# Three orders in a two-block transformer kernel: convolution taps in other loops around the gates, a merge tile's high and low parts at the head of the next step, key reciprocals spread by transpositions

## The chip, the cores and the metric

The kernel runs on one core of one Trainium2 chip. The metric is the device time of one execution in microseconds (us); smaller is better. The engines are TensorE (PE; its weight loads are listed apart, as PEld), VectorE (DVE), ScalarE (ACT), GpSimd (POOL) and the queue of SyncE (SP), which issues most of the transfers.

## What is computed

Two transformer blocks on 512 positions of width 1024. Cut to the parts that the change touches:

```python
# first block, token mixer
z = h @ w_in + b_in
q, k, v, glu_a, glu_b, gate_a, gate_b = jnp.split(z, splits, axis=-1)
a = chunked_rel_attention(q, k, v, rel_bias) @ w_attn_o
u = glu_a * jax.nn.sigmoid(glu_b)                    # 512 channels
u = causal_dwconv(u, w_dw, b_dw)                     # 31 taps in each channel
u = jax.nn.silu(layer_norm(u, g_ln, b_ln))
cb = u @ w_conv_o + b_conv_o
y = jax.nn.sigmoid(gate_a) * a + jax.nn.sigmoid(gate_b) * cb
return y @ w_mix_o
# second block, recurrence: keys divided by their norm in each head
kk = hd(k * k_k)
kk = kk / jnp.maximum(jnp.sqrt(jnp.sum(kk * kk, axis=-1, keepdims=True)), 1e-12)
# second block, merge of its two branches: again sigmoid(gate) * branch, summed, then a 1024x1024 product
```

Everything is float32. A large product is made of three passes of a faster format: both operands are cut into a high part and a low rest, and the matmuls high x high, high x low and low x high are added.

## The kernel before

All activations are kept with channels on the 128 partitions and the 512 positions along the row, so a width of 1024 is 8 tiles (DT = 8). Weights come in units of 128x1024 (one output tile of a product) through a ring of four slots; a slot's next load is issued when PE has used the unit in it. ACT or POOL makes a unit's high part and POOL its low part. The instruction stream of each engine is written out by hand, and the engines meet only through semaphores; what stands in a row on one engine runs in that order, and a wait holds back all that is behind it.

**Front and convolution (40 to 150 us).** PE makes the 8 tiles of the gated linear unit, then 12 units of queries, keys and values. `gate(g)` exists on ACT (the sigmoid) and on DVE (the product and the first tap with the bias). It is there for four tiles of channels, 0 to 3. Channels 1, 2 and 3 take their 30 further taps on DVE: `tap` is one `scalar_tensor_tensor` on a PSUM bank that must wait for the tap before it in the same channel; `taps_on(n, *channels)` is a loop of n rounds with one tap for each channel named, as (channel, first tap). Channel 0 takes 26 taps in pairs whose products ACT makes (`act_tap_pair`) and POOL adds (`pool_tap_pair`), and its last four on DVE (L1188). Then DVE sums the channels (L1197 to L1203), PE adds over partitions with a matrix of ones (L977), DVE centres (L1208), ACT squares, DVE sums again (L1213), PE's second L977 follows, then root and reciprocal (L1216). PE stands behind both L977: the first is behind unit 9 of the 12, the second behind unit 10. DVE also has four modulation products (L1444) between L1213 and L1216. Attention begins on PE at L689, behind unit 11.

**Merges (`act_mix`, `dve_mix`, `pe_mix`).** For each of 8 tiles n PE makes four half or whole products in PSUM, ACT two sigmoids (L1495), DVE two products and their sum y[n] (L1526, L1528, L1531). `first_part(n)` on ACT makes the high part Y_HI (L1488), `second_part(n)` on DVE the low part Y_LO (L1519). In the first block's merge ACT also makes high parts of weights (L866) and DVE four modulation products a step. The product that follows (mixo1, mixo2) reads y tile by tile: `pe_first_units_split` does tiles 0 to 6 of unit 0, then two tiles of unit 1, then tile 7 of unit 0, and `y_ready(k)` is its wait ahead of tile k of unit 0.

**Recurrence, preparation (`pe_rprep`, 826 to 982 us).** For each of 8 tiles PE makes three units (L2349 to L2351) and between them small products: `key_spread(j)` turns DVE's reciprocals, laid out by position, back to channels with four 128x128 matmuls against the identity (L2326). DVE's L2477 waits for them.

Of the kernel before, what the change touches and what calls it, by code (L numbers as in the profile page):

```python
# [181 lines left out]
def build_program(nc, stream, cols, const, onehot, c_rows, x_t, mem_t, line1, table2, w2a2, g2, cmp_w2, out, scratch, rows):  # L182

    with ExitStack() as ctx:
# [677 lines left out]
        def act_front_high(act, u):  # L862

            slot = u % W_SLOTS
            act.wait_ge(w_full[slot], 16 * (u // W_SLOTS + 1))
            nc.scalar.activation(FHI[:, slot, :], W[:, slot, :], ACT.Copy).then_inc(f_whi, 1)  # L866
# [115 lines left out]
        def act_front(act):  # L982
# [46 lines left out]
            act.dma_start(scratch[1, 0:H2, :], line2[:, 0:LINE]).then_inc(s_line2, 16)  # L1029
            for n in range(4):  # L1030
                act_tap_pair(act, n)
            gate(2)
            act_front_high(act, 4)
            act_tap_pair(act, 4)
# [62 lines left out]
        def dve_front(dve):  # L1097
# [80 lines left out]
            gate(1)  # L1178
            taps_on(10, (1, 1))
            gate(2)  # L1180
            taps_on(10, (1, 11))
            gate(3)
            taps_on(10, (1, 21), (2, 1), (3, 1))
            taps_on(20, (2, 11), (3, 11))
            for t in range(TAIL_TAPS):
                at = CONV_K - TAIL_TAPS + t
                dve.wait_ge(l_vec, t) if t else dve.wait_ge(s_cv[0], 1)
                V.scalar_tensor_tensor(psum[0][:, :], GLU[:, 0, LEAD - CONV_K + 1 + at:LEAD - CONV_K + 1 + at + S],  # L1188
                                       prm("w_dw_conv", at), psum[0][:, :], ALU.mult, ALU.add).then_inc(l_vec, 1)
# [286 lines left out]
        def act_mix(act, stage, per, bias_a, bias_b, y, hi):  # L1476
# [12 lines left out]

            for n in range(DT):  # L1490
                act.wait_ge(s_ev, e0 + n - 1)
                for h, bias in enumerate((bias_a, bias_b)):
# [4 lines left out]
                    if per == 3 and n < DT - 1:  # L1497
                        for m in ((4,), (5, 6))[h]:
                            if 3 * n + m < 3 * DT:
                                act_front_high(act, u0 + 3 * n + m)  # L1500
                if n:
                    first_part(n - 1)
                if per == 3 and n + EARLY < ADA_LATE // 4:
# [6 lines left out]
        def dve_mix(dve, stage, per, y, bias, hi, lo):  # L1510
# [9 lines left out]

            for n in range(DT):
                dve.wait_ge(s_glu, g0 + 2 * n + 2)
                dve.wait_ge(unit_done, u0 + per * (n + 1))
                t = SQ[:, 2 * (n % 2), :]
                v = SQ[:, 2 * (n % 2) + 1, :]
                nc.vector.tensor_tensor(t, psum[4 * (n % 2) + 1][:, :], t, ALU.mult).then_inc(s_dve, 1)  # L1526
                b = 0.0 if bias is None else prm(bias, n)
                nc.vector.scalar_tensor_tensor(v, psum[4 * (n % 2) + 3][:, :], b, v, ALU.add, ALU.mult)\  # L1528
                    .then_inc(s_dve, 1)
                dve.wait_ge(s_dve, d0 + 2 * (n + 1) + max(0, n - 1))  # L1530
                nc.vector.tensor_tensor(y[n], t, v, ALU.add).then_inc(s_ev, 1)  # L1531
                if n:
                    second_part(n - 1)
                if per == 3 and n + EARLY < ADA_LATE // 4:
                    late_modulation(dve, n + EARLY)
# [171 lines left out]
        def pe_ffn1(pe):  # L1707
            mixed = BASE["mix1"]

            def y_ready(k):  # L1710
                pe.wait_ge(s_dve, mixed.dve + min(3 * k + 5, 3 * DT))

# [599 lines left out]
        def pe_rprep(pe):  # L2312
# [10 lines left out]
            def key_spread(j):  # L2323
                pe.wait_ge(m_rec, j + 1)
                for b in range(S // P):
                    last = nc.tensor.matmul(psum[5][:, b * P:(b + 1) * P], TMP[7][:, b * P:(b + 1) * P], con("ident"),  # L2326
                                            start=True, stop=True)
                last.then_inc(m_wide, 1)
# [459 lines left out]
        def pe_cross(pe):  # L2788
            base, mixed = BASE["cross"], BASE["mix2"]

            def y_ready(k):
                pe.wait_ge(s_dve, mixed.dve + 2 * DT + min(3 * k + 5, 3 * DT))

# [708 lines left out]
```

## Time and profile before

| | |
|---|---|
| time, median of 3 runs | 2260.36 us (2259.55 to 2262.89) |
| profiled execution, its own time | 2267.29 us |
| its span | 2265.5 us |
| PE busy | 2201.3 us, 97% of the span |
| DVE, ACT, POOL busy | 1162.1, 775.2, 1211.4 us |
| mean granted clock of TensorE | 0.992 of full speed |

An engine is busy while an instruction of it runs; matmuls are pipelined, so their listed length (0.39 us) is more than the distance between the starts of two of them (0.23 us for 512 columns). A row of a timeline gives start, length, engine, line and instruction, and in brackets the idle time ahead of it with what ended that time.

### The profile page before, as it was taken

The page shows a single profiled execution, that of the slowest core. Times are in us where ns is not written, and L with a number is a line of the kernel's source. Part 1 is how long each engine was busy: PE and PEld are TensorE (multiplying, and loading weights), DVE is VectorE, ACT ScalarE, POOL GpSimd, SP SyncE. Part 2 cuts the span into 40 slices and gives each one's busy share as a digit, 9 for nine tenths or more (in the row PEclk, how much of TensorE's full clock was granted, in tenths as well). Part 3 has the DMA queues.
Part 4 walks back from the last instruction along what each step waited for, and adds up shares of the span by engine and source line. Part 5 has one row for each costly group of instructions (what it writes and reads, how often), then busy time and mean ns, then how long its engine had stood idle before and what let it go on. Part 6 is the DMA issues. An engine that isn't in the chain of part 4 may idle for free.

```text
span 2265.5 us, 40352 instructions
## 1 busy us (share of the span) xinstructions
PE 2201.3 (97%) x16228; PEld 1730.8 (76%) x16228; DVE 1162.1 (51%) x1719; ACT 775.2 (34%) x1355; POOL 1211.4 (53%) x681
## 2 busy tenths in 40 slices
PE   9989999999999999998879998999999999999999
PEld 4857877888888767788876575668887788888887
DVE  7885656555520467753335526673217637555500
ACT  5455322433310266533324225771002242323200
POOL 1955454688877300000006454568877458777776
PEclk9989999999999999999999998999999999999999
DMA  8533652333323332220002240002334212323322
GB/s 330 165 133 112 234 194 84 116 102 93 97 97 93 98 125 75 84 79 4 4 4 75 75 168 19 2 1 93 101 95 137 84 48 93 101 93 100 95 93 102
DMA packets 65425, 220.77 MB, mean 97 GB/s; under 512 B 6913, under 2 KB 9226, under 8 KB 65282
## 3 DMA queue, kind: packets, MB, share of 16 engines
q1 hardware_dynamic: 51072, 179.81, 24.6%
q10 hardware_dynamic: 9986, 24.82, 3.0%
q0 software_dynamic: 4224, 14.06, 1.8%
q8 instruction: 111, 1.82, 0.3%
q14 instruction: 32, 0.26, 0.0%
HBM read 213.09 MB, written 11.86 MB: 99 GB/s over the span
## 4 chain that ended last, share of the span: by engine, by line
PE 73%; POOL 11%; issue 9%; DVE 5%; ACT 1%; DMA 1%; DVEq 0%; POOLq 0%; SPq 0%; ACTq 0%
PE banks L498 12%; PE banks L499 12%; PE banks L500 12%; POOL WH L451 5%; POOL WL_A L454 3%; PE banks L2113 3%; PE banks L2068 3%; PE banks L746 2%; PE banks L689 2%; PE banks L707 2%; PE banks L2349 2%; PE banks L2350 2%; PE banks L2351 2%; PE banks L905 2%; PE banks L906 2%
## 5 line engine op out<-in xcount | busy, mean ns | idle before, releaser
L451 POOL TENSOR_TENSOR WH<-W,ZERO 128x1024 fp32r<-128x1024 f32 x194 | 368.6, 1900 | 280.2 <-PE banks L500 247.3
L454 POOL TENSOR_TENSOR WL_A<-W,WH 128x1024 fp32r<-128x1024 f32 x138 | 339.4, 2460 | 10.9
L498 PE MATMUL banks<-HF,WH 128*128 128x512 f32 x704 | 275.9, 392 | 0.1
L499 PE MATMUL banks<-HF,WH 128*128 128x512 f32 x704 | 273.9, 389 | 0.0
L500 PE MATMUL banks<-HF,WL_A 128*128 128x512 f32 x704 | 273.9, 389 | 0.0
L488 POOL TENSOR_TENSOR WH<-W,ZERO 128x1024 fp32r<-128x1024 f32 x20 | 41.2, 2058 | 277.8 <-DVEq L399 204.6
L872 POOL TENSOR_TENSOR WR_LO<-W,FRONT_HI 128x1024 fp32r<-128x1024 f32 x40 | 96.0, 2406 | 128.8 <-ACT FRONT_HI L866 87.2
L498 PEld LDWEIGHTS banks<-HF,WH 128*128 128x128 f32 x704 | 132.2, 188 | 28.2 <-POOL WL_A L454 0.5
L500 PEld LDWEIGHTS banks<-HF,WL_A 128*128 128x128 f32 x704 | 132.2, 188 | 27.6
L499 PEld LDWEIGHTS banks<-HF,WH 128*128 128x128 f32 x704 | 132.2, 188 | 27.3 <-issue 0.2
L454 POOL TENSOR_TENSOR WL_C<-W,WH 128x1024 fp32r<-128x1024 f32 x56 | 141.7, 2530 | 4.4
L498 PE MATMUL banks<-HID,WH 128*128 (+1 forms) x352 | 137.4, 390 | 0.9 <-POOL WL_A L454 0.9
L499 PE MATMUL banks<-HID,WH 128*128 (+1 forms) x352 | 137.0, 389 | 0.0
L500 PE MATMUL banks<-HID,WL_A 128*128 (+1 forms) x352 | 136.9, 389 | 0.0
L1639 DVE TENSOR_TENSOR HID<-SQ,HID 128x512 f32 x44 | 98.0, 2227 | 41.0 <-ACT HID L1596 41.0
L498 PE MATMUL banks<-HN_HI,WH 128*128 128x512 f32 x288 | 115.6, 402 | 0.8 <-issue 0.4
L499 PE MATMUL banks<-HR,WH 128*128 128x512 f32 x288 | 112.3, 390 | 0.0
L1617 DVE SCALAR_TENSOR_TENSOR SQ<-banks,PRM,SQ 128x511 f32<-128x511 f32 x66 | 49.4, 748 | 115.2 <-ACT SQ L1589 114.6
L3234 POOL DMA_DIRECT2D BIG<-g x1 | 0.5, 532 | 198.0 <-DVEq L399 198.0
L1589 ACT ACTIVATE SQ<-banks,PRM 128x512 f32<-128x512 f32 x66 | 51.2, 776 | 127.5 <-PE banks L500 84.3
L844 POOL TENSOR_SCALAR BIG<-BIG,SM,GT 128x128 f32<-128x128 f32 (+3 forms) x96 | 60.7, 644 | 57.6 <-DVE SM L806 57.6
L1526 DVE TENSOR_TENSOR SQ<-banks,SQ 128x512 f32<-128x512 f32 x16 | 11.1, 691 | 154.7 <-PE banks L500 123.8
(499 smaller groups left out, 5333.0 us busy)
## 6 DMA issues: line engine op xcount, KB each, us to landing
W<-stream SPq DMA_DIRECT2D x308, 512.0 KB, 3.5
BIG<-stream ACTq DMA_DIRECT2D x30, 512.0 KB, 5.3
BIG<-stream SPq DMA_DIRECT2D x20, 512.0 KB, 11.4
bias_rows<-bias_lines POOLq DMA_DIRECT2D x1, 4096.0 KB, 18.9
X<-x_t SPq DMA_DIRECT2D x2, 1024.0 KB, 7.6
BIG<-stream SPq DMA_DIRECT2D x2, 1024.0 KB, 11.8
bias_rows<-bias_lines POOLq DMA_DIRECT2D x1, 2048.0 KB, 16.1
BIG<-bias_rows POOLq DMA_DIRECT2D x1, 2048.0 KB, 11.2
```

Source lines behind the costliest of these rows:

```text
L451: nc.gpsimd.tensor_tensor(WH[:, half, :], W[:, slot, :], ZERO[:, 0:1].to_broadcast([P, D]), ALU.add)\
L454: nc.gpsimd.tensor_tensor(WL[stage][half], W[:, slot, :], WH[:, half, :], ALU.subtract)\
L498: nc.tensor.matmul(out_ap, w_hi, hi, start=start, stop=False)
L499: nc.tensor.matmul(out_ap, w_hi, lo, start=False, stop=False)
L500: return nc.tensor.matmul(out_ap, w_lo, hi, start=False, stop=stop)
L844: ins = nc.gpsimd.tensor_scalar(p, p, SM[:, 32 + m:33 + m], part["gate"][c], ALU.mult, ALU.mult)
L872: nc.gpsimd.tensor_tensor(WR_LO[:, slot, :], W[:, slot, :], FHI[:, slot, :], ALU.subtract).then_inc(f_wlo, 1)
L1589: nc.scalar.activation(SQ[:, 2 * j + h, :], psum[2 * j + h][:, :], ACT.Identity, scale=taps(w, off + j, i, 2), bias=PRM[:, bass.ds(C0[b] + ...
L1617: nc.vector.scalar_tensor_tensor(t[:, 1:S], bank[:, 0:S - 1], taps(w, off + j, i, 1), t[:, 1:S], ALU.mult, ALU.add).then_inc(s_dve, 1)
L1639: nc.vector.tensor_tensor(HIDS[1][:, 2 * i + j, :], SQ[:, 2 * j, :], HIDS[0][:, 2 * i + j, :], ALU.subtract).then_inc(s_ev, 2)
L2068: return nc.tensor.matmul(out_ap[to:to + CHUNK, :], lhs(at, j), rhs(at, j), start=start, stop=stop)
L2113: last = nc.tensor.matmul(one_bank(b)(j)[lo:lo + CHUNK, :], lhs[1](lo, j), rhs[1](lo, j), start=True, stop=True)
```

## The change

On DVE the rounds of the tap loops are distributed otherwise, and five taps of channel 3 stand singly between the last four of channel 0. On ACT two tap pairs go behind the sigmoid of gate 2. In the merges the high and low parts of tile n-1 stand at the head of step n, and PE's wait for tile k asks for the parts up to k. The four matmuls of the key spread become four transpositions.

```diff
@@ act_front
-            for n in range(4):
+            for n in range(2):
                 act_tap_pair(act, n)
             gate(2)
+            for n in range(2, 4):
+                act_tap_pair(act, n)
             act_front_high(act, 4)
@@ dve_front
             gate(1)
-            taps_on(10, (1, 1))
+            taps_on(11, (1, 1))
             gate(2)
-            taps_on(10, (1, 11))
+            taps_on(5, (1, 12), (2, 1))
             gate(3)
-            taps_on(10, (1, 21), (2, 1), (3, 1))
-            taps_on(20, (2, 11), (3, 11))
-            for t in range(TAIL_TAPS):
+            taps_on(14, (1, 17), (2, 6), (3, 1))
+            taps_on(11, (2, 20), (3, 15))
+            for t in range(TAIL_TAPS + 1):
+                tap(3, CONV_K - TAIL_TAPS, t)
+                if t == TAIL_TAPS:
+                    break
@@ act_mix
             for n in range(DT):
+                if n:
+                    first_part(n - 1)
                 act.wait_ge(s_ev, e0 + n - 1)
...
-                if n:
-                    first_part(n - 1)
@@ dve_mix
             for n in range(DT):
+                if n:
+                    second_part(n - 1)
                 dve.wait_ge(s_glu, g0 + 2 * n + 2)
...
-                dve.wait_ge(s_dve, d0 + 2 * (n + 1) + max(0, n - 1))
+                dve.wait_ge(s_dve, d0 + 2 * (n + 1) + n)
                 nc.vector.tensor_tensor(y[n], t, v, ALU.add).then_inc(s_ev, 1)
-                if n:
-                    second_part(n - 1)
@@ y_ready, for mixo1 (and the same for mixo2)
-                pe.wait_ge(s_dve, mixed.dve + min(3 * k + 5, 3 * DT))
+                pe.wait_ge(s_dve, mixed.dve + 3 * (k + 1))
@@ key_spread
-                    last = nc.tensor.matmul(psum[5][:, b * P:(b + 1) * P], TMP[7][:, b * P:(b + 1) * P], con("ident"),
-                                            start=True, stop=True)
+                    last = nc.tensor.transpose(psum[5][:, b * P:(b + 1) * P], TMP[7][:, b * P:(b + 1) * P], con("ident"))
```

On ACT, in the front, before. The rows of L880 are the tap pairs' products (two instructions a pair), L1018 the sigmoids of gates 2 and 3, L866 high parts of weights:

```order
L1029 DMA bias_lines<-BIG 16x640
L880 ACTIVATE BIG<-BIG,PRM 128x512 x8
L1018 ACTIVATE SQ<-banks,PRM 128x512
L866 ACTIVATE FRONT_HI<-W 128x1024
L880 ACTIVATE BIG<-BIG,PRM 128x512 x2
```

and of the change:

```order
L1029 DMA bias_lines<-BIG 16x640
L880 ACTIVATE BIG<-BIG,PRM 128x512 x4
L1018 ACTIVATE SQ<-banks,PRM 128x512
L880 ACTIVATE BIG<-BIG,PRM 128x512 x4
L866 ACTIVATE FRONT_HI<-W 128x1024
```

Two of the four pairs ahead of gate 2's sigmoid are now behind it.

On DVE, at the end of the second block's merge, before (L1526 and L1528 are the two products, L1531 is y, Y_LO the low part; the last L1531 is of tile 7):

```order
L1531 TENSOR_TENSOR BIG<-SQ 128x512
L1519 TENSOR_TENSOR Y_LO<-BIG,Y_HI_97 128x512
L1526 TENSOR_TENSOR SQ<-banks,SQ 128x512
L1528 SCALAR_TENSOR_TENSOR SQ<-banks,SQ 128x512
L1531 TENSOR_TENSOR BIG<-SQ 128x512
L1519 TENSOR_TENSOR Y_LO<-BIG,Y_HI_98 128x512
L1519 TENSOR_TENSOR Y_LO<-BIG,Y_HI_99 128x512
```

and of the change:

```order
L1538 TENSOR_TENSOR BIG<-SQ 128x512
L1524 TENSOR_TENSOR Y_LO<-BIG,Y_HI_98 128x512
L1533 TENSOR_TENSOR SQ<-banks,SQ 128x512
L1535 SCALAR_TENSOR_TENSOR SQ<-banks,SQ 128x512
L1538 TENSOR_TENSOR BIG<-SQ 128x512
L1524 TENSOR_TENSOR Y_LO<-BIG,Y_HI_99 128x512
```

The low part of tile 6 (Y_HI_98) stood behind the y of tile 7 and now stands ahead of tile 7's products.

## Rows read from the trace of the kernel before

**Rows 1.** Timeline of PE, 120 to 152 us, matmuls behind unit 9.

```profile
126.36 0.39 PE L907 MATMUL banks<-H_HI,WR_LO 128*128 128x512 f32 x1
...
132.85 2.08 PE L977 MATMUL banks<-SQ,CON 128*128 128x512 f32 x2 [6.11 <-DVE SQ L1203]
133.94 1.42 PE L905 MATMUL banks<-H_HI,FRONT_HI 128*128 128x512 f32 x1
...
135.58 0.63 PE L907 MATMUL banks<-H_HI,WR_LO 128*128 128x512 f32 x1
...
141.41 1.02 PE L977 MATMUL banks<-SQ,CON 128*128 128x512 f32 x2
...
147.84 1.58 PE L689 MATMUL banks<-BIG 64*128 64x128 f32 x12
```

**Rows 2.** Windows: PE, PEld, DVE, ACT, POOL busy; granted clock; DMA share, GB/s.

```profile
129.00:132.00 3.00, 0.00 (x0) 0.00 (x0) 2.73 (x5) 1.19 (x2) 0.00 (x0) 0.74 1.01 274
...
135.00:138.00 3.00, 3.00 (x10) 2.29 (x10) 3.00 (x5) 2.31 (x4) 0.00 (x0) 0.62 1.06 386
```

**Rows 3.** Timeline of DVE, 40 to 165 us.

```profile
62.72 0.76 DVE L1164 SCALAR_TENSOR_TENSOR banks<-BIG,PRM,banks 128x512 f32<-128x512 f32 x1 [0.18 <-DVE banks L1164]
67.82 0.75 DVE L1155 SCALAR_TENSOR_TENSOR BIG<-banks,PRM,SQ 128x512 f32<-128x512 f32 x1 [4.34 <-ACT SQ L1018]
...
69.33 0.75 DVE L1164 SCALAR_TENSOR_TENSOR banks<-BIG,PRM,banks 128x512 f32<-128x512 f32 x1
...
79.91 46.18 DVE L1164 SCALAR_TENSOR_TENSOR banks<-BIG,PRM,banks 128x512 f32<-128x512 f32 x70
125.99 3.14 DVE L1188 SCALAR_TENSOR_TENSOR banks<-BIG,PRM,banks 128x512 f32<-128x512 f32 x4
...
137.37 2.27 DVE L1213 TENSOR_TENSOR SQ<-banks,SQ 128x512 f32<-128x512 f32 x3
...
144.33 3.35 DVE L1216 RECIPROCAL ST<-ST 128x512 f32<-128x512 f32 x1
148.95 0.29 DVE L794 CUSTOM_DVE_ANT_0 BIG<-banks,BIG 128x128 f32<-128x128 f32 x1 [1.27 <-PE banks L689]
```

**Rows 4.** Timelines around gates 2 and 3: PE, then ACT.

```profile
64.00 1.98 PE L966 MATMUL banks<-HR,FRONT_HI 128*128 128x512 f32 x8
...
64.57 2.56 ACT L880 ACTIVATE BIG<-BIG,PRM 128x512 f32<-128x512 f32 x4 [9.40 <-POOL BIG L888]
...
71.45 0.69 ACT L1018 ACTIVATE SQ<-banks,PRM 128x512 f32<-128x512 f32 x1 [1.57 <-PE banks L969]
```

**Rows 5.** Timelines at the end of the first merge: PE, DVE, ACT.

```profile
326.83 0.50 PE L498 MATMUL banks<-Y_HI,WH 128*128 128x512 f32 x1 [1.57 <-DVE Y_LO L1519]
...
329.02 0.39 PE L498 MATMUL banks<-Y_HI,WH 128*128 128x512 f32 x1
...
323.33 2.85 DVE L1531 TENSOR_TENSOR BIG<-SQ 128x512 f32<-128x512 f32 x1
326.10 1.47 DVE L1519 TENSOR_TENSOR Y_LO<-BIG,Y_HI 128x512 fp32r<-128x512 f32 x2
...
326.21 0.63 ACT L1488 ACTIVATE Y_HI<-BIG 128x512 fp32r<-128x512 f32 x1 [3.78 <-DVE BIG L1531]
```

**Rows 6.** Timelines at the end of the second merge: PE, POOL.

```profile
1704.83 0.50 PE L498 MATMUL banks<-Y_HI,WH 128*128 128x512 f32 x1 [1.29 <-DVE Y_LO L1519]
...
1701.52 2.71 POOL L454 TENSOR_TENSOR WL_C<-W,WH 128x1024 fp32r<-128x1024 f32 x1
```

**Rows 7.** Timeline of PE: a key spread and what follows; transpositions in both attentions.

```profile
892.27 1.06 PE L2326 MATMUL banks<-CON,BIG 128*128 128x128 f32 x8
893.09 0.48 PE L2349 MATMUL banks<-XR,WR_HI 128*128 128x512 f32 x1
...
149.35 1.97 PE L854 MATMUL banks<-CON,BIG 128*128 128x128 f32 x16
...
1492.88 0.66 PE L707 MATMUL banks<-CON,BIG 128*128 128x128 f32 x4
```

More of the change, by code:

```diff
@@ L2791, in y_ready @@
             def y_ready(k):
-                pe.wait_ge(s_dve, mixed.dve + 2 * DT + min(3 * k + 5, 3 * DT))
+                pe.wait_ge(s_dve, mixed.dve + 2 * DT + 3 * (k + 1))
             def sums(n, bank, width, first, last):
```

## The prediction

> **What bounds the kernel now.** I read the page first: PE is busy for 2201.3 of 2265.5 us, so a microsecond counts only where PE itself stops or where PE's own work shrinks. I then asked who PE waited for, stage by stage, and opened the timelines at the places that the change touches. Three of them matter. Behind unit 9 of the queries, keys and values PE has its longest wait, 6.11 us for the last of DVE's channel sums (L1203), and its next matmuls run on half the clock [rows 1]. At the end of both merges PE stops before the high and low parts of y, for some 1.5 us each [rows 5, 6]. In the preparation of the recurrence PE has no gap, so its key spreads are paid in full [rows 7]. Between 40 and 126 us, and inside both merges, no wait of PE is listed at all.
>
> **The convolution.** DVE's chain is what ends PE's wait, so its length is what to work out. A tap alone costs 0.76 + 0.18 = 0.94 us, since it waits for the tap before it; 70 taps in rounds of two or three cost 46.18 us, 0.66 each; the four tail taps, single, 3.14 us, 0.785 each; the gate's pair of instructions is 69.33 - 67.82 = 1.51 us; and DVE stands idle for 4.34 us ahead of gate 2 [rows 3]. That idle time is ACT's doing: its sigmoid for gate 2 stands behind four tap products that had waited for POOL until 64.57 [rows 4]. What the sigmoid needs otherwise is PE's unit 1, which ends where the third unit's part at 64.00 has displaced it. I place it by gate 3, whose sigmoid begins at 71.45, two units later; two units are four groups of eight matmuls, 1.81 us each by the distance of such groups, so 7.25 us, and gate 2's sigmoid can begin at 64.20 [rows 4]. With 0.69 us for it and 0.1 to DVE, gate 2 starts there at 64.98 in place of 67.82.
>
> DVE by the new order: ten single taps ended with the one at 62.72; the eleventh begins at 63.66 and ends at 64.42, so it fits ahead of the gate. Gate 2 takes until 66.49; five rounds of two, 6.6 us, until 73.1; gate 3 (its sigmoid is ready at 72.1) until 74.6; 14 rounds of three and 11 of two are 64 taps, 42.2 us, until 116.8; the nine taps of the tail alternate between two channels, so I take 0.66 for each, 5.9 us, until 122.8. Before, the tail ended at 129.1 [rows 3]. The chain is 6.3 us shorter, and it comes from the idle time (2.8 us), from nine single taps that now have company (2.5 us) and from the tail, about 1 us after rounding.
>
> PE would then get its sums at 132.85 - 6.3 = 126.55, and its unit 9 ends at 126.36 + 0.23 = 126.59 [rows 1]. The gap of 6.11 us closes to 0 to 0.3. With it goes its echo: granted clock 0.74 while PE stood, and 0.62 from 135 to 138 [rows 2]; the matmuls there lie 0.43 us apart and not 0.23. From the start of the first L977 to the start of the second, one pair of L977 and one unit, it took 141.41 - 132.85 = 8.56 us; the same pair and a unit from the second L977 to attention took 147.84 - 141.41 = 6.43, at the full clock [rows 1]. So 2.1 us more. This stage: 6.1 + 2.1 = 8.2 us.
>
> Does the rest keep up? The second L977 would start at 126.6 + 6.4 = 133.0. DVE's squares ended at 137.37 + 2.27 = 139.6; they move with the first sums and with the faster first L977 (about 0.8 us), to 132.5. In time, by 0.5 us. Then modulation, 4.7 us, and the reciprocal, 3.35 us, end at 140.6; before they ended at 147.7 and DVE waited 1.27 us for attention's first scores [rows 3], which now come at 148.95 - 8.2 = 140.75. So DVE's slack is spent almost to zero: more than 8.4 us cannot be had here, and each microsecond by which DVE or ACT is late behind the sums comes off. Costs that I put at nothing: the two pairs behind the sigmoid begin 0.3 us later than before (64.9 for 64.57), and POOL, which adds them, has a finish some 6 us ahead of DVE's need; the sigmoid of gate 3 waits for PE in any case [rows 4]. If that cover were gone it would cost the same 0.3 us. The part is worth 8.2 us, between 5 (DVE's loops or its later chain 3 us slower than drawn) and 8.4.
>
> **The merges.** The same number of instructions runs; only tile 6's parts leave the end. First merge: PE waits 1.57 us for the low part of tile 6 and begins it at 326.83; the last tile of unit 0 begins at 329.02, without a wait [rows 5]. Now tile 6 goes on at once and PE arrives at tile 7 at 329.02 - 1.73 = 327.3 (the wait with its restart). But tile 7's parts are late next: y ends at 326.1, Y_HI at 326.84, one Y_LO, half of the 1.47 us for two, at about 327.55 [rows 5]. So PE stops there 0.25 us, and 1.5 us are gained. Second merge: the gap was 1.29 us plus the 0.16 us of a cold start. The next thing late is the second unit's low weights, which POOL ends at 1701.52 + 2.71 = 1704.23 [rows 6]; PE, without its gap, wants them at 1704.06. Gain 1.3 us. Together 2.8, between 1.5 (DVE slowed by POOL on the new places of Y_LO) and 3.2. In the seven steps before the end, ACT's high part now waits for y ahead of the sigmoids; y is ready 16 us or more before PE needs that bank again, so I cost it at nothing.
>
> **The key spread.** Four matmuls show as eight instructions and hold PE for 893.09 - 892.27 = 0.82 us. Sixteen transpositions in attention, sixteen instructions in the trace, take 1.97 us, so four take 0.47 to 0.49; four others show 0.66 us against the spread's 1.06 by the same measure [rows 7]. So 0.35 to 0.40 us is saved in each of 8 spreads: 2.8 us, with 0 and 3.3 as bounds (nothing, if the distance there is set by weight loads; halving the whole 0.82). DVE's wait for the spread only gets shorter.
>
> The Trainium skill ("TensorE: Matmul & The Clock Gate", Back-to-back issue gap) gives about 81 ns for each weight load with a matmul of 128 columns in a stream. By it four instructions less would save 0.32 us a spread, 2.6 us in all; the rows say 0.10 us an instruction and 2.8, and the sum goes by the rows.
>
> **Sum.** 8.2 + 2.8 + 2.8 = 13.8 us. The profiled execution has 2267.3 us of its own; it would be 2253.5. It lies 6.9 us above the median of the runs, in which I expect the same waits. So 2260.4 - 13.8 = **2246.6 us**.
>
> **The rivals.**
> *The chain behind the sums takes the place of the wait.* The sums come early, but ACT's copies, the squares, the modulation or the reciprocal arrive 3 to 6 us late, or PE's clock falls in attention in place of here. For it: DVE's slack ahead of attention is only 1.27 us [rows 3], and transfers filled the engines from 129 to 138 us [rows 2]. Against it: in the trace none of these steps waits for a transfer. With 4.5 us lost, 2251.1.
> *The transpositions do not do what they are for.* If their distance is that of the matmuls they replace: 13.8 - 2.8 = 11.0, so 2249.4. Against it, the eight records for four matmuls and sixteen for sixteen transpositions [rows 7].
> *The convolution brings nothing.* Something else holds PE at 126.6, a weight unit's low part or a bank. Then 5.6 us remain, 2254.8. Speaks against it: PE's restart has one releaser, L1203 [rows 1].
> *Slower.* Each spread by transpositions lets the clock fall behind it. After the long wait the clock was at half for some 6.6 us, 130.7 to 137.3 (drawn from [rows 1, 2]), 3.3 us lost. Eight such falls are 26.4 us: 2246.6 + 26.4 = 2273.0. It decides from 1.75 us lost per spread. The rows speak against it: the clock fell only after a wait of microseconds, and a spread is 0.5 us amid 20 us of dense matmuls.
> The Trainium skill ("TensorE: Matmul & The Clock Gate", Part 4: PE-mode transpose) says that a transposition does not count as work for the clock gate. That is what this rival would need; no row of the preparation holds a transposition before the change.
>
> **How the numbers follow.** Forecast 0.63; chain behind the sums 0.17; transpositions alike 0.08; convolution nothing 0.05; two of the parts failing together, within 0.2% of before, 0.04; slower 0.03. The forecast's own range is 2244 to 2249. The bounds of the parts reach from 13.8 + 1.1 = 14.9 us gained (with the scatter of the runs, 2243.5) to the chain's loss, 2251.1 and its upper half, 2253.5; what lies outside is the nothing-cases and the worst of the first rival. A change of 0.2% (4.5 us) is about what a measurement of this kernel tells from none. Faster 0.92, same 0.05, slower 0.03.
>
> **What would show it.** After the change: gate 2 on DVE at about 65 us without 4 us of idle time; the tail's end near 122.8; PE's first L977 near 126.6 with no gap, and a granted clock of 1.00 from 126 to 140; L689 near 139.6; at the end of each merge no wait at tile 6 and at most 0.5 us at tile 7; four records a spread and 0.45 to 0.5 us between its start and the next L2349. The prediction is wrong if the alternating tail runs at the pace of single taps, if DVE's squares come after 133, or if a wait of the same length turns up at the start of attention.

## The result, and the profile after

| kernel | median, us | lowest to highest | runs | ratio to before, 95% |
|---|---|---|---|---|
| before | 2261.82 | 2259.55 to 2270.87 | 5 | |
| after | 2251.47 | 2246.78 to 2255.57 | 5 | 0.9943 [0.9924, 0.9961] |

The change makes the kernel faster by 0.57%; on 2261.8 us the ratio is 12.9 us, from 8.8 to 17.2. The two medians lie 10.4 us apart, the spans of the two profiled executions 11.7 (2265.5 and 2253.8).

The page of the kernel after begins so; PE is busy for 2.9 us less than before and the span is 11.7 us shorter, so 8.8 of the 11.7 us are time in which PE had stood (64.2 us of the span before, 55.4 now).

```profile
span 2253.8 us, 40281 instructions
PE 2198.4 (98%) x16196; PEld 1729.8 (77%) x16196; DVE 1147.9 (51%) x1719; ACT 776.3 (34%) x1355; POOL 1214.9 (54%) x681
```

The timeline of DVE in the convolution, from gate 2 to attention's first scores, answers to [rows 3]:

```profile
63.93 0.76 DVE L1166 SCALAR_TENSOR_TENSOR banks<-BIG,PRM,banks 128x512 f32<-128x512 f32 x1 [0.18 <-DVE banks L1166]
65.24 0.75 DVE L1157 SCALAR_TENSOR_TENSOR BIG<-banks,PRM,SQ 128x512 f32<-128x512 f32 x1 [0.55 <-ACT SQ L1018]
...
74.84 43.02 DVE L1166 SCALAR_TENSOR_TENSOR banks<-BIG,PRM,banks 128x512 f32<-128x512 f32 x65
...
122.37 0.75 DVE L1166 SCALAR_TENSOR_TENSOR banks<-BIG,PRM,banks 128x512 f32<-128x512 f32 x1
123.03 0.68 DVE L1202 TENSOR_TENSOR SQ<-BIG,banks 128x512 f32<-128x512 f32 x1
...
130.41 2.27 DVE L1218 TENSOR_TENSOR SQ<-banks,SQ 128x512 f32<-128x512 f32 x3
...
137.18 3.35 DVE L1221 RECIPROCAL ST<-ST 128x512 f32<-128x512 f32 x1
140.84 0.29 DVE L794 CUSTOM_DVE_ANT_0 BIG<-banks,BIG 128x128 f32<-128x128 f32 x1 [0.32 <-PE banks L689]
```

The 4.34 us of idle time ahead of gate 2 are 0.55, the rounds run at 43.02 / 65 = 0.66 us a tap, and the alternating tail keeps that pace (122.37 to 123.03). The last bracket is DVE's slack ahead of attention: 0.32 us where it was 1.27.

PE over the same stretch, against [rows 1], and then its windows, with the columns of [rows 2]:

```profile
126.84 1.13 PE L977 MATMUL banks<-SQ,CON 128*128 128x512 f32 x2
127.41 0.79 PE L905 MATMUL banks<-H_HI,FRONT_HI 128*128 128x512 f32 x1
...
133.30 1.02 PE L977 MATMUL banks<-SQ,CON 128*128 128x512 f32 x2
...
139.73 1.58 PE L689 MATMUL banks<-BIG 64*128 64x128 f32 x12
```

```profile
129.00:132.00 3.00, 3.00 (x15) 2.47 (x14) 2.79 (x6) 2.13 (x4) 0.00 (x0) 1.00 0.99 248
...
147.00:150.00 3.00, 1.88 (x8) 1.55 (x10) 2.96 (x8) 2.91 (x8) 2.55 (x3) 0.52 0.00 0
```

Neither L977 has a wait in brackets any more, PE is busy for all 3 us of 129 to 132 where it stood still, and the granted clock there is 1.00 in place of 0.74. But the last row has a granted clock of 0.52 inside attention. It is no new fall: the kernel before had one too, some 10 us behind its own first scores (its window is below), and the matter returns further on.

```profile
159.00:162.00 3.00, 1.93 (x14) 1.59 (x15) 2.60 (x11) 2.74 (x11) 2.96 (x2) 0.50 0.00 0
```

The ends of the merges, against [rows 5] (PE, DVE, ACT) and [rows 6] (PE, then POOL):

```profile
318.37 0.50 PE L498 MATMUL banks<-Y_HI,WH 128*128 128x512 f32 x1 [0.28 <-DVE Y_LO L1524]
...
317.62 0.69 DVE L1524 TENSOR_TENSOR Y_LO<-BIG,Y_HI 128x512 fp32r<-128x512 f32 x1 [0.70 <-ACT Y_HI L1493]
...
316.96 0.63 ACT L1493 ACTIVATE Y_HI<-BIG 128x512 fp32r<-128x512 f32 x1 [4.31 <-DVE BIG L1538]
```

```profile
1693.69 0.50 PE L498 MATMUL banks<-Y_HI,WH 128*128 128x512 f32 x1
...
1690.91 2.73 POOL L454 TENSOR_TENSOR WL_C<-W,WH 128x1024 fp32r<-128x1024 f32 x1
```

One Y_LO in place of two stands behind the last y, and PE waits 0.28 us, at tile 7. In the second merge no wait is listed; PE restarts at 1693.69, and POOL's low weights ended at 1690.91 + 2.73 = 1693.64.

A key spread and what follows it, the timeline of PE against [rows 7]:

```profile
880.35 0.60 PE L2331 MATMUL banks<-CON,BIG 128*128 128x128 f32 x4
880.70 0.48 PE L2353 MATMUL banks<-XR,WR_HI 128*128 128x512 f32 x1
```

Four records, 0.35 us from start to start, where eight took 0.82.

### The profile page after: what moved, and what is told of

Its sections match the earlier page's. It is cut to its first block, busy times and chain, and to the rows that moved or that the text cites. A ratio compares the mean times of both kernels' runs of the same rounds, so it can differ in the third digit from the quotient of the medians.

```text
span 2253.8 us, 40281 instructions
## 1 busy us (share of the span) xinstructions
PE 2198.4 (98%) x16196; PEld 1729.8 (77%) x16196; DVE 1147.9 (51%) x1719; ACT 776.3 (34%) x1355; POOL 1214.9 (54%) x681
## 4 chain that ended last, share of the span: by engine, by line
PE 76%; POOL 11%; issue 8%; DVE 3%; ACT 1%; DMA 1%; POOLq 0%; SPq 0%; DVEq 0%; ACTq 0%
PE banks L498 12%; PE banks L500 12%; PE banks L499 12%; POOL WH L451 5%; POOL WL_A L454 3%; PE banks L2118 3%; PE banks L2073 3%; PE banks L689 2%; PE banks L707 2%; PE banks L905 2%; PE banks L907 2%; PE banks L746 2%; PE banks L906 2%; PE banks L2353 2%; PE banks L2354 2%
## 5 line engine op out<-in xcount | busy, mean ns | idle before, releaser
L498 PE MATMUL banks<-HF,WH 128*128 128x512 f32 x704 | 275.9, 392 | 0.1
L498 PEld LDWEIGHTS banks<-HF,WH 128*128 128x128 f32 x704 | 132.1, 188 | 28.2 <-POOL WL_A L454 0.5
L498 PE MATMUL banks<-HID,WH 128*128 (+1 forms) x352 | 137.4, 390 | 0.9 <-POOL WL_A L454 0.9
L498 PE MATMUL banks<-HN_HI,WH 128*128 128x512 f32 x288 | 115.6, 401 | 0.8 <-issue 0.4
L1533 DVE TENSOR_TENSOR SQ<-banks,SQ 128x512 f32<-128x512 f32 x16 | 11.1, 691 | 149.3 <-PE banks L500 121.0
## 6 DMA issues: line engine op xcount, KB each, us to landing
BIG<-stream SPq DMA_DIRECT2D x2, 1024.0 KB, 11.7
BIG<-bias_rows POOLq DMA_DIRECT2D x1, 2048.0 KB, 10.9
```

What stands on the lines that cost most here:

```text
L498: nc.tensor.matmul(out_ap, w_hi, hi, start=start, stop=False)
```

## The experiments

Each of the twelve runs was profiled once and timed against the kernel before, on three occasions: the first four, the next four, the last four. Two of them are the kernels after and before once more, and one repeats another run. The median of before was 2264.70 (26 runs), 2264.25 (27 runs) and 2264.23 us (17 runs) on them. Since the times of single executions scatter by 5 us and more, I read each trace at fixed places too. This table is worked out from the starts of instructions: how much earlier (-) or later each execution reached a place than the profiled execution of before did.

| kernel | first L977 (132.9) | scores L689 (147.8) | behind attention (187) | behind merge 1 (330) | ahead of the spreads (825) | behind them (983) | ahead of the last chunk (1161) | behind it (1189) | 1396 | ahead of the end of merge 2 (1700) | behind it (1708) | end |
|---|---|---|---|---|---|---|---|---|---|---|---|---|
| after | -6.1 | -8.1 | -9.2 | -10.5 | -10.6 | -14.1 | -14.1 | -10.7 | -10.6 | -10.6 | -11.8 | -11.8 |
| e1_conv | -6.5 | -8.5 | -9.0 | -9.1 | -9.1 | -9.1 | -9.1 | -5.4 | -7.7 | -7.8 | -7.8 | -7.7 |
| e2_merge | -0.1 | -0.2 | -0.2 | -1.5 | -1.5 | -1.6 | -3.9 | 0.0 | -2.1 | -2.2 | -3.4 | -3.3 |
| e3_turn | 0.2 | 0.8 | -1.2 | -1.2 | -1.2 | -4.9 | -2.9 | -3.3 | -6.1 | -6.2 | -6.2 | -6.2 |
| e4_no_turn | -6.3 | -8.4 | -9.6 | -10.9 | -11.0 | -11.0 | -9.4 | -9.8 | -12.3 | -12.4 | -13.6 | -13.5 |
| e5_act_only | -3.1 | -3.5 | -4.7 | -4.7 | -4.7 | -4.8 | -7.7 | -8.8 | -11.1 | -11.1 | -11.1 | -11.0 |
| e6_loops_only | -3.5 | -5.5 | -7.6 | -7.6 | -7.6 | -7.7 | -7.7 | -6.3 | -9.3 | -9.3 | -9.3 | -9.3 |
| e7_after_again | -6.0 | -8.0 | -10.1 | -11.4 | -11.4 | -15.0 | -16.1 | -13.9 | -14.6 | -14.6 | -15.8 | -15.8 |
| e8_before_again | 0.0 | 0.2 | -1.9 | -1.9 | -1.9 | -1.9 | -4.9 | -5.1 | -7.6 | -7.7 | -7.6 | -7.6 |
| e9_fill | -6.2 | -8.2 | -9.2 | -10.5 | -10.5 | -14.2 | -16.3 | -13.2 | -15.4 | -15.4 | -16.6 | -16.6 |
| e10_late | -6.1 | -8.2 | -6.9 | -8.2 | -8.3 | -11.9 | -12.9 | -8.4 | -10.5 | -10.6 | -11.8 | -11.7 |
| e11_fill_again | -6.1 | -8.1 | -9.2 | -10.6 | -10.6 | -14.2 | -16.0 | -12.6 | -15.1 | -15.2 | -16.4 | -16.4 |
| e12_before_fill | 0.1 | -0.4 | -0.7 | -0.7 | -0.7 | -0.8 | -2.9 | -0.5 | -2.6 | -2.7 | -2.7 | -2.6 |

A column is read against the one before it. Where the change acts, the step is the same within 0.2 us in every kernel that has that part (0.5 for the convolution) and within 0.1 us of 0 in those that have not; only ahead of the scores do kernels with the old convolution scatter by up to 0.8. Elsewhere steps of up to 5 us come between kernels that are alike there. The last chunk of the recurrence, in which PE does only six steps that wait for one another, begins at 1173.8 us in the kernel before, so behind the column 1161.

### The parts alone

**e1_conv** has the convolution's part of the diff alone:

```diff
-            for n in range(4):
+            for n in range(2):
                 act_tap_pair(act, n)
             gate(2)
+            for n in range(2, 4):
+                act_tap_pair(act, n)
...
-            taps_on(10, (1, 1))
+            taps_on(11, (1, 1))
...
-            for t in range(TAIL_TAPS):
+            for t in range(TAIL_TAPS + 1):
+                tap(3, CONV_K - TAIL_TAPS, t)
```

> The convolution's part alone (ACT's tap pairs behind gate 2, DVE's loops and tail). Theory: the first L977 on PE starts near 126.8 us with no gap, attention (L689) near 139.8 us against 147.8, and the whole 8 to 9.3 us that the changed kernel showed at the end of attention stays to the end of the kernel; timed 8 to 9 us faster. Rival (the falls of the granted clock take part of it back elsewhere): the same start of attention, but the trace shows a later stage, the end of the recurrence above all, in which more than 2 us go, and the time is only 4 to 6 us faster.

Measured: 2258.41 us (9 runs), ratio 0.9966 [0.9953, 0.9978], which is 7.7 us (5.0 to 10.6). The trace has the scores 8.5 us earlier. Behind them only stages that differ between alike kernels move it: 3.7 us are lost at the end of the recurrence, where the granted clock is 0.68 from 1165 to 1175 us and 0.50 from 1175 to 1185, and 2.3 come back up to 1396 us. That is what the rival expected of the trace; of the time it expected a gain of 4 to 6 us, the theory 8 to 9, and the interval holds both.

**e2_merge** has the merges' part alone:

```diff
             for n in range(DT):
+                if n:
+                    first_part(n - 1)
                 act.wait_ge(s_ev, e0 + n - 1)
...
             for n in range(DT):
+                if n:
+                    second_part(n - 1)
                 dve.wait_ge(s_glu, g0 + 2 * n + 2)
```

> The merges' part alone. Theory: 1.2 us at the end of each merge, PE's wait for tile 6 gone and one of 0.3 us at tile 7 of the first; timed 2.4 us faster. Rival (moving the parts costs something in the seven steps before): less than 1.5 us in all, and the step of 16.3 us in the first merge grows.

Measured: 2260.34 us, 0.9985 [0.9975, 0.9995], 3.4 us (1.1 to 5.7). By the table 1.3 us in the first merge (0.2 to 1.5) and 1.2 in the second (2.2 to 3.4).

**e3_turn** has the transpositions alone, **e4_no_turn** everything but them:

```diff
-                    last = nc.tensor.matmul(psum[5][:, b * P:(b + 1) * P], TMP[7][:, b * P:(b + 1) * P], con("ident"),
-                                            start=True, stop=True)
+                    last = nc.tensor.transpose(psum[5][:, b * P:(b + 1) * P], TMP[7][:, b * P:(b + 1) * P], con("ident"))
```

> The transpositions alone. Theory: 0.44 us in each of 8 spreads, 3.5 us less from the first spread to the end of the preparation; timed 3.5 us faster. Rival (transpositions let the granted clock fall): the clock falls in the preparation or at the end of the recurrence, near 1180 us, and 4 us are given back there; timed 0 to 1 us faster.

> Convolution and merges without the transpositions. Theory (the 4 us that the changed kernel lost at the end of the recurrence are a fall of the clock that comes and goes by execution): 10.6 us off at the start of the preparation, and 10 to 11.7 us off in time. Rival (the transpositions brought that fall): no fall of the clock in the last chunk of the recurrence in any execution, and the time is the same as that of the changed kernel or better.

Measured: e3_turn 2260.93 us, 0.9977 [0.9965, 0.9989]; e4_no_turn 2253.73 us, 0.9952 [0.9937, 0.9968]. Over the preparation, from 825 to 983 us, e3_turn gains 3.7 us (1.2 to 4.9) and e4_no_turn 0.0. The spread in e3_turn reads as in the kernel after (timeline of PE):

```profile
889.62 0.60 PE L2326 MATMUL banks<-CON,BIG 128*128 128x128 f32 x4
889.97 0.48 PE L2348 MATMUL banks<-XR,WR_HI 128*128 128x512 f32 x1
```

So the rivals in which the transpositions bring nothing, or make the clock fall behind each spread, are out: the gain is there when they stand alone and gone when they alone are missing, and the granted clock of e3_turn from 825 to 979 us is 1.00. A fall of the clock at the end of the recurrence, which I had seen in the kernel after and half suspected of them, is not theirs either: it is as long, and costs 3.7 and 3.9 us (1161 to 1189 in the table), in e1_conv and e2_merge, which have no transposition there, and e3_turn, which has them, loses nothing. In e4_no_turn the clock falls too, for a shorter time (0.66 from 1175 to 1185 us).

### What the convolution's gain is made of

**e5_act_only** has only the move of ACT's tap products behind the sigmoid of gate 2, **e6_loops_only** only DVE's new loops: its diff is e1_conv's without the first hunk.

```diff
-            for n in range(4):
+            for n in range(2):
                 act_tap_pair(act, n)
             gate(2)
+            for n in range(2, 4):
+                act_tap_pair(act, n)
```

> Only ACT's two tap pairs behind gate 2; DVE's loops as before. Theory: gate 2 starts on DVE at 65.2 us (67.8 before), the sums end 2.9 us earlier, PE's wait at the first L977 is 3.2 us. If the clock falls behind that wait as before, the stage gains 2.9 us; if a wait of 3.2 us does not let it fall, 5.0 us. Rival (ACT's order buys nothing because gate 2 is bound by PE or POOL): less than 1 us.

> Only DVE's loops and tail; ACT's order as before. Theory: gate 2 stays at 67.8 us, with 3.4 us of idle time ahead of it; the sums end 3.5 us earlier, PE's wait is 2.6 us; the stage gains 3.5 us with the clock's fall, up to 5.6 without. Rival (the loops bring all of it): 6 us or more.

Measured: e5_act_only 2261.91 us (10 runs), 0.9989 [0.9977, 1.0001]; e6_loops_only 2259.72 us (10 runs), 0.9982 [0.9971, 0.9993]. The ratios don't part the two, and the first does not exclude that nothing was gained; the traces part them. PE's timeline in e5_act_only:

```profile
129.83 1.12 PE L977 MATMUL banks<-SQ,CON 128*128 128x512 f32 x2 [3.46 <-DVE SQ L1205]
130.39 0.80 PE L905 MATMUL banks<-H_HI,FRONT_HI 128*128 128x512 f32 x1
131.04 0.59 PE L906 MATMUL banks<-HR,FRONT_HI 128*128 128x512 f32 x1
131.42 0.63 PE L907 MATMUL banks<-H_HI,WR_LO 128*128 128x512 f32 x1
```

and in e6_loops_only:

```profile
129.43 1.13 PE L977 MATMUL banks<-SQ,CON 128*128 128x512 f32 x2 [2.68 <-DVE SQ L1206]
129.99 0.79 PE L905 MATMUL banks<-H_HI,FRONT_HI 128*128 128x512 f32 x1
130.62 0.39 PE L906 MATMUL banks<-HR,FRONT_HI 128*128 128x512 f32 x1
130.84 0.39 PE L907 MATMUL banks<-H_HI,WR_LO 128*128 128x512 f32 x1
```

The wait of 6.11 us became 3.46 with the move and 2.68 with the rounds: they take off 2.7 and 3.4, 6.1 together, so both parts of the prediction's account hold and they add up. The echo does not divide that way. Behind 3.46 us of standing, matmuls follow one another after 0.43 us and the granted clock from 132 to 135 us is 0.59; behind 2.68 us they follow after 0.23 and it is 1.00. So the rounds alone gain 3.5 + 2.0 = 5.5 us at the scores, and the move alone 3.1 + 0.4. One execution of each shows this; the wait of 6.1 us, which five executions have (before, e2_merge, e3_turn, e8_before_again and e12_before_fill), brought the fall in all five.

### The same kernels once more

The falls of the clock differed so much between the first traces that I profiled and timed the kernels after and before a second time, unchanged.

> The changed kernel once more, unchanged. Theory (a fall of the clock in the last chunks of the recurrence is an event of the execution): offsets to the kernel before are again -8.1 us at attention, -10.6 at the end of mixo1's first units and -14.1 at the first chunk, and the loss at the end of the recurrence is of another size, 0 to 4 us. Rival (it belongs to the change): the loss is again 3 to 4 us at the same place.

> The kernel before once more, unchanged, for the scatter of one kernel against itself. Theory: ratio 1.000 within 0.2%, all stages alike within 0.3 us but for those in which the granted clock is below 1: those at 125 to 137 us, at the start of attention, at the end of the recurrence and near 1370 us differ by 1 to 4 us from one execution to another.

Measured: e7_after_again 2251.49 us, 0.9938 [0.9924, 0.9951], 14.0 us (11.1 to 17.2); e8_before_again 2262.38 us, 0.9997 [0.9987, 1.0007]. The two profiled executions of after differ by 4.1 us in their spans, those of before by 7.6, and the table shows where: between the scores and 187 us, in the chunks of the recurrence and their end, and between 1365 and 1396 us. All are places where PE is fed in short pieces and stops between them. They are not all the clock's doing.

- From the scores to 187 us it is the clock. The three executions without a fall there (e3_turn, e6_loops_only, e8_before_again) take 37.3 us, and so does e7_after_again with a short one; the ten others take 38.1 to 39.3 (e10_late, whose DVE is late there, 40.6), before 39.3 and after 38.2. So e7_after_again is at -11.4 and -15.0 us behind the first merge and the key spreads, where -10.6 and -14.1 were expected.
- From 983 to 1161 us it is not. The granted clock is 1.00 in both executions of before, which take 178.0 and 175.0 us; PE's stops that the profile puts down to "issue", in which it waited for nothing that the profile shows, add up to 17.4 us in the one and 14.4 in the other. The expectation, which had all the scatter in places where the clock is below 1, missed this. Over all executions the stage takes 175.0 to 179.9 us.
- Between 1365 and 1396 us it is the clock again. The windows of the two executions of before, first the one the prediction was made from:

```profile
1380.00:1390.00 10.00, 9.49 (x33) 4.17 (x32) 7.21 (x20) 6.90 (x18) 6.81 (x10) 0.50 0.00 0
1390.00:1400.00 10.00, 9.27 (x74) 6.77 (x72) 6.63 (x33) 5.10 (x17) 7.15 (x7) 0.83 0.01 2
```

```profile
1370.00:1380.00 10.00, 7.97 (x22) 3.74 (x23) 10.00 (x32) 7.72 (x27) 6.65 (x10) 0.66 0.00 0
1380.00:1390.00 10.00, 8.09 (x74) 4.94 (x73) 7.44 (x29) 6.99 (x21) 6.71 (x9) 1.00 0.00 0
```

The same program is on half the clock for more than ten microseconds in the one and for some seven in the other, which runs 5 to 8 us ahead at that place. So a step of 2 or 3 us in those stretches is no effect of an edit, and one pair of profiles cannot weigh this change to better than some 5 us, though it can weigh each part where it acts.

### Can the clock be held by filler matmuls?

In the kernel after the clock fell at the end of the recurrence, to half for 20 us. Windows:

```profile
1165.00:1175.00 10.00, 6.73 (x160) 6.20 (x160) 1.81 (x3) 0.60 (x1) 0.00 (x0) 0.50 0.01 2
1175.00:1185.00 10.00, 8.43 (x64) 3.95 (x57) 6.09 (x9) 1.97 (x4) 4.25 (x2) 0.51 0.01 2
```

**e9_fill** (and **e11_fill_again**, the same) puts ten matmuls on zeros, into a bank that nothing reads, in the waits of the last chunk of the kernel after; **e12_before_fill** puts them into the kernel before.

```diff
+                        if c == N_CH:
+                            for _ in range({1: 2, 5: 3, 6: 2}.get(n, 1)):
+                                nc.tensor.matmul(psum[2][:, :], ZERO[:, 3:4].to_broadcast([P, P]),
+                                                 ZERO[:, 3:4].to_broadcast([P, S]), start=True, stop=True)
```

> The changed kernel, and in the last chunk of the recurrence, where PE does only the six steps that wait for one another, ten matmuls of zeros into a bank that is free there, placed in PE's waits (0.46 us each at the full clock; their result is not used). Theory (the clock falls there because PE has little work between its waits): the granted clock stays at 1.00 until the next stage, the two steps behind the fifth take 0.8 us and not 1.0 to 3 us, and the loss of 1 to 4 us at the end of the recurrence is gone: L2551 starts 14 to 15 us ahead of the kernel before, and the time is 2 us better than the changed kernel's. Rival (the fall is not set by PE's work there): the clock falls at the same place, and the fillers, at half the clock, make the stage 1 to 3 us longer.

> The kernel with the ten fillers once more, for a second profile: by the theory the clock is at 1.00 in the last chunk here too; by the rival it falls in at least one of the two.

> The kernel before with the same ten fillers. Theory: the stage from the last chunk to the input of the next takes as long as in the execution of before with the latest fall, or up to 4 us less; the time is 1 to 3 us better than before. Rival: 1 to 3 us worse.

Measured: e9_fill 2252.40 us, 0.9950 [0.9935, 0.9964]; e11_fill_again 2251.77 us, 0.9947 [0.9933, 0.9961]; e12_before_fill 2267.48 us, 1.0011 [1.0000, 1.0023]. The kernel after without them had 0.9943 and 0.9938: no gain, and in the kernel before a loss of 2.5 us (0 to 5.2), as its rival had named. Yet the clock was held: from 1145 to 1195 us it is at 1.00 in all three, and each of the eleven executions without fillers has a fall there. Windows, and PE's timeline, of e9_fill:

```profile
1165.00:1175.00 10.00, 10.00 (x206) 6.01 (x204) 2.68 (x5) 0.60 (x1) 0.00 (x0) 1.00 0.02 4
1175.00:1185.00 10.00, 8.79 (x23) 3.67 (x22) 8.18 (x11) 3.24 (x6) 4.25 (x2) 1.00 0.00 0
```

```profile
1175.51 1.12 PE L2555 MATMUL banks<-BIG,CON 1*128 1x512 f32 x2
1176.56 3.70 PE L2569 MATMUL banks<-BIG,CON 128*128 128x512 f32 x8
1180.56 0.47 PE L498 MATMUL banks<-HN_HI,WH 128*128 128x512 f32 x1 [0.30 <-DVE HR L2715]
...
1181.72 0.50 PE L498 MATMUL banks<-HN_HI,WH 128*128 128x512 f32 x1 [0.24 <-DVE HR L2715]
```

against the kernel after, where the first two lines are L2551 and L2565:

```profile
1178.03 2.07 PE L2551 MATMUL banks<-BIG,CON 1*128 1x512 f32 x2 [1.57 <-DVEq L399]
1180.03 6.04 PE L2565 MATMUL banks<-BIG,CON 128*128 128x512 f32 x8
1185.51 0.79 PE L498 MATMUL banks<-HN_HI,WH 128*128 128x512 f32 x1
1186.14 0.39 PE L499 MATMUL banks<-HR,WH 128*128 128x512 f32 x1
```

The traces tell where it went. Two things take it.

The first is the fillers' own length. From the second of the six steps to L2551 PE takes 11.9 us where the clock is at 1.00 through the steps and there is no filler (before, e3_turn, e5_act_only, e8_before_again) and 12.2 to 12.3 in three more (e7_after_again among them, with 12.26); it takes 16.0 to 16.3 in the four executions in which the clock is down for 20 us (after, e1_conv, e2_merge, e10_late); and 14.36 in all three with fillers. A step with one filler is 2.13 us long for 1.85 to 1.95, and the one with three is 4.79 for 3.40. So the fillers save 1.6 to 2.0 us where the long fall would have come and cost 2.1 to 2.5 where it would not, which is the more frequent case here. That is why the kernel before, whose clock was at 1.00 in these steps in both executions without fillers, only lost. Fillers no longer than the waits were not tried.

The second is the stage behind. In e9_fill PE is through the eight instructions behind L2555 in 3.70 us in place of 6.04 and begins L498 4.95 us ahead of the kernel after (1180.56 for 1185.51), when it was 2.5 ahead at L2555 (1175.51 for 1178.03; 13.2 ahead of the kernel before, for 14 to 15 expected). But now it waits seven times, 2.0 us in all, for DVE's HR, a tile of which comes every 1.26 us, and at 1230 us it is 2.5 ahead again. From L2551 (L2547 in before) to the same instruction near 1230 us (L2577 in before, at 1240.66) it is 51.9 to 52.0 us in all fourteen executions, whatever the clock was: DVE sets the pace there, and what half the clock takes from PE is not lost.

### DVE's slack ahead of attention

The prediction put DVE's slack at the first scores near zero in the kernel after, and the profile puts it at 0.32 us. **e10_late** makes DVE 3.3 us late there, by a second reciprocal ahead of L1221:

```diff
+            V.reciprocal(SQ[:, 3, :], ST[:, 1, :])
```

> The changed kernel with one more reciprocal of 128x512 on DVE (3.35 us, its result is not used) between the modulation and the reciprocal that attention needs. Theory (DVE's chain behind the sums had 0.3 us of slack left, as the trace of the changed kernel shows it waiting for L689): attention's first scores are read 3.0 us later, and the time is 3 us longer. Rival (there is other slack in attention, so that PE does not feel it): less than 1 us longer at the end of attention.

Measured: 2251.17 us (4 runs), 0.9940 [0.9924, 0.9956], no longer than the kernel after. But the trace shows the cost where it was expected. DVE's timeline, then PE's:

```profile
137.02 3.35 DVE L1221 RECIPROCAL SQ<-ST 128x512 f32<-128x512 f32 x1
140.28 3.29 DVE L1222 RECIPROCAL ST<-ST 128x512 f32<-128x512 f32 x1
143.61 0.29 DVE L794 CUSTOM_DVE_ANT_0 BIG<-banks,BIG 128x128 f32<-128x128 f32 x1
```

```profile
144.31 1.95 PE L689 MATMUL banks<-BIG 64*128 64x512 f32 x8 [1.27 <-DVE SM L794]
148.20 0.98 PE L689 MATMUL banks<-BIG 64*128 64x128 f32 x4 [1.94 <-DVE SM L794]
```

DVE's first step on the scores comes 2.77 us later (143.61 for 140.84) without idle time ahead of it, PE has a new wait of 1.27 us behind it and one of 1.94 in place of 0.53, and at 187 us this execution is 2.3 us behind the kernel after. The clock falls in attention for the same time in both, so this is the delay itself. By 1396 us the two are level again, over the stretches that scatter. So the slack is spent, as read. The expected 3 us in time were not measured: 2.3 us are 0.10%, and the interval is 0.16% to either side, so these timings neither show nor exclude them.

## Why the prediction was right, and what was off

**The time.** 2246.6 us was forecast and 2251.47 measured, inside the range of 2243.5 to 2253.5. The size of the gain was nearly right: 13.8 us forecast, 12.9 (8.8 to 17.2) and 14.0 (11.1 to 17.2) by the two ratios. What was off was the base, in the step "So 2260.4 - 13.8": three runs had put before at 2260.4; with two more, of 2261.8 and 2270.9, the five have it at 2261.8, and the samples of 17 to 27 runs at 2264.2 to 2264.7. From 2264.3 the same sum would have given 2250.5.

**The sum, part by part**, at the places where each part acts:

| part | forecast | after | e7_after_again | alone |
|---|---|---|---|---|
| convolution, to the scores | 8.2 | 8.1 | 8.0 | 8.5 |
| first merge | 1.5 | 1.3 | 1.3 | 1.3 |
| eight key spreads | 2.8 | 3.5 | 3.6 | 3.7 |
| second merge | 1.3 | 1.2 | 1.2 | 1.2 |
| sum | 13.8 | 14.1 | 14.1 | 14.7 |

**The convolution.** Gate 2 began on DVE at 65.24 for 64.98, the tail ended near 123.1 for 122.8, the first L977 began at 126.84 for 126.6, the second at 133.30 for 133.0, the scores at 139.73 for 139.6: the whole chain came 0.1 to 0.3 us behind the drawing. The split into idle time and company for single taps is borne out by e5_act_only and e6_loops_only. That DVE's later work would keep up, with almost nothing to spare, is borne out by the squares (132.7 for 132.5), the slack of 0.32 us and e10_late.

**The echo.** 2.1 us for the clock after the long wait was right in size: from the first L977 to the second it is 6.46 us for 8.56. What I had not seen is that it may hang on the wait's length in a jump: it was gone with 2.68 us of wait and nearly whole with 3.46. If that holds, a change that takes 3 us off the wait is worth 3 or 5; one execution of each length is all there is for it.

**The merges.** Tile 6 goes on at once and tile 7 waits 0.28 us, for 0.25 forecast; in the second merge PE restarts 0.05 us behind POOL's low weights, which was named as the next thing late. The gains are 0.2 and 0.1 us under the forecast.

**The key spread** is the term that was mis-sized, and beyond its own upper bound of 3.3 us. I took 0.47 us for four transpositions, from sixteen in attention and from groups that stand between other work [rows 7]. In the preparation four take 0.35 us from start to start; 0.82 - 0.35 = 0.47 a spread, and 3.5 to 3.7 by the table for eight. The bound "halving the whole 0.82" took the eight records as the only thing that shrinks; a transposition's record is also closer to the next one there, 0.088 us for 0.103.

**The rivals.** *Transpositions alike* and *slower by falls of the clock* fell to e3_turn and e4_no_turn, *the convolution brings nothing* to e1_conv. *The chain behind the sums* is the one that stood close: it did not happen, but e10_late shows that 2.8 us more on DVE cost 2.3 at the end of attention. Its second form, a fall of the clock in attention in place of here, took nothing from the gain, because the kernel before has that fall as well (0.50 from 159 to 162 us; after, 0.52 from 147 to 150). Of the five executions with the old convolution three have it and two have not, and all seven with the whole of the new one have it, one of them shorter. So the change does not bring it, but whether it makes it more frequent is not shown; an execution without it passes attention 1 to 2 us faster.

Against *slower* the prediction says that the clock fell only after a wait of microseconds. That was misread: in the kernel before it also fell in attention, behind waits of 0.52 and 1.76 us, at the end of the recurrence and near 1380 us. The rival is out by what e3_turn measured, not by that sentence.

**What stays open.** The falls of the clock and PE's issue stops in the recurrence are worth some 5 us between executions; what makes them come in one execution and not in the next no run shows, and whether the change alters how often they come can't be told from so few profiles. That the wait's length is what decides over the echo stands on one execution of each kernel. The sum of the parts timed alone, 7.7 + 3.4 + 5.2 = 16.3 us, lies above the 12.9 and 14.0 of the whole, within intervals that are each 2 to 3 us wide to either side.

## What to carry to other kernels

Work out the chain of the engine that releases the wait, instruction by instruction, and then the slack of the next meeting of the two engines: the first gave this gain to 0.3 us, the second says where to stop. Judge a gain of 0.1 to 0.5% by the starts at fixed places on both sides of the edit, profile the unchanged kernel twice to learn which stretches scatter by themselves, and take the base from many runs, since here it was off by 3.9 us, more than the merges or the key spreads were worth. Filling PE's waits did hold its clock, but here it paid nothing: the fillers were longer than the waits, and in the work that followed DVE and not PE set the pace.

## What the runs showed of the hardware

- **Taps in a chain.** A tap that reads what the tap before it wrote starts 0.94 us after it, with 0.18 us of idle time; with another channel in between, the distance is 0.66, and two channels taking turns are enough.
- **The clock and the length of a wait.** Behind a wait of 2.68 us the granted clock stayed at 1.00 (2.4 GHz), behind 3.46 us it was 0.59 from 132 to 135 us, and with 6.11 us it fell while PE still stood (0.74 from 129 to 132 us) and was 0.62 from 135 to 138; a value between 0.50 (1.2 GHz) and 1.00 is a window that holds both levels. A long wait is not needed: in attention the clock fell to 0.50 behind waits of 0.52 and 1.76 us in the kernel before. Such falls in stretches of short pieces come and go between executions of one program.
- **Zeros hold the clock.** Ten matmuls on zeros in PE's waits kept the granted clock at 1.00 at the end of the recurrence in three executions of three; without them it fell in eleven of eleven.
- **Two readers of SBUF.** In the profile after, 111 TENSOR_TENSOR instructions of DVE with both operands in SBUF start more than 0.2 us before the end of one of POOL, and each ends 0.54 to 0.56 us behind that end, however early it started; the 32 that read one operand from PSUM instead take 0.68 to 0.70 us as ever. In the second merge after, DVE's timeline has

```profile
1690.28 1.09 DVE L1538 TENSOR_TENSOR BIG<-SQ 128x512 f32<-128x512 f32 x1
1692.08 2.10 DVE L1524 TENSOR_TENSOR Y_LO<-BIG,Y_HI 128x512 fp32r<-128x512 f32 x1 [0.70 <-ACT Y_HI L1493]
```

where POOL's instructions end at 1690.82 (1688.93 + 1.89) and 1693.64. The first ends at 1691.37 and the second at 1694.18, 0.55 and 0.54 later; the same Y_LO takes 0.69 us at 317.62, where POOL is idle. The Trainium skill ("SBUF — State Buffer", SBUF: two separate sides) states such an exclusive lock for a DVE operation with two SBUF inputs beside one of GpSimd that reads SBUF, and these rows agree. It is why the low parts of y cost DVE 2 us or 0.7 by their place. The prediction had this as its lower bound for the merges; it did not reach PE.
